# Negated scores with an exponential for each score map, and a later wait inside the transposes, in a hybrid attention and expert layer

## The reference, cut to what matters

```python
def diff_attention(q, k, v, lam):
    scale = dh ** -0.5                      # dh = 64, so an eighth
    ...
        s = jnp.einsum('bqhcd,bkhcd->bchqk', qblk, k).astype(F32) * scale
        p = jax.nn.softmax(s, axis=-1)
        a = p[:, 0] - lam * p[:, 1]
        return jnp.einsum('bhqk,bkhe->bqhe', a, vf)
```

## Time and profile before

| | us |
|---|---|
| three runs | 1222.29, 1220.74, 1217.69 |
| median | 1220.74 |
| the profiled execution, whole | 1222.5 |
| its span, first to last instruction | 1220.7 |
| PE busy in the span | 1082.9 (89%) |
| DVE busy | 595.6 (49%) |
| ACT busy | 404.4 (33%) |
| attention, half 0 | from 372 to 556 |
| attention, half 1 | from 641.7 to 783.3 |

### The profile page before, as it was taken

One profiled execution on the slowest core, in us unless ns is written; L12 is line 12 of the kernel. 1 busy time (PEld: TensorE's weight loads), 2 busy tenths in 40 slices (PEclk: granted clock), 3 DMA queues, 4 the chain that ended last, 5 costly groups with the idle time before them and its releaser, 6 DMA issues.

```text
span 1220.7 us, 13833 instructions
## 1 busy us (share of the span) xinstructions
PE 1082.9 (89%) x5427; PEld 776.9 (64%) x5427; DVE 595.6 (49%) x929; ACT 404.4 (33%) x799; POOL 103.5 (8%) x108
## 2 busy tenths in 40 slices
PE   4999999989998999999998899799994899777775
PEld 2687777777886777777876677687884333323322
DVE  4478525647335455451545665465639522222126
ACT  4441131112145555552236555431322111111103
POOL 1000011111000000000000101000014111111002
PEclk9999999989999999999999999899996899999998
DMA  9747723221421312313221211465519899999966
GB/s 307 264 165 259 261 97 108 83 61 52 147 87 36 111 53 65 109 52 129 70 86 53 63 56 52 165 262 192 209 47 333 350 420 420 420 421 419 418 269 239
DMA packets 72707, 226.17 MB, mean 185 GB/s; under 512 B 9534, under 2 KB 20087, under 8 KB 59331
## 3 DMA queue, kind: packets, MB, share of 16 engines
q1 hardware_dynamic: 65106, 208.35, 46.2%
q0 software_dynamic: 4464, 10.12, 2.2%
q10 hardware_dynamic: 3072, 6.82, 1.5%
HBM read 205.68 MB, written 25.72 MB: 190 GB/s over the span
## 4 chain that ended last, share of the span: by engine, by line
PE 66%; DVE 10%; issue 10%; ACT 9%; DMA 3%; SPq 1%; POOL 1%; ACTq 0%; DVEq 0%; POOLq 0%
PE ps L1084 36%; PE ps L1320 10%; PE ps L1333 5%; PE ps L1244 3%; ACT arena L1647 3%; DMA arena<-in_w_ada 2%; PE ps L1274 2%; PE ps L1038 2%; ACT w_high L1465 1%; PE ps L1258 1%; DVE mx L2122 1%; PE ps L1313 1%; DVE w_low L1825 1%; PE ps L1115 1%; DVE mx L2123 1%
## 5 line engine op out<-in xcount | busy, mean ns | idle before, releaser
L1084 PE MATMUL ps<-w_high,h_high 128*128 128x512 f32 x600 | 242.1, 403 | 5.4 <-DVE arena L1938 2.5
L1084 PE MATMUL ps<-w_high,h_low 128*128 128x512 f32 x600 | 235.8, 393 | 0.0
L1084 PE MATMUL ps<-w_low,h_high 128*128 128x512 f32 x600 | 235.7, 393 | 0.0
L1825 DVE TENSOR_TENSOR w_low<-w_loaded,w_high 128x2048 fp32r<-128x2048 f32 x44 | 100.7, 2289 | 105.9 <-ACT w_high L1465 105.9
L1320 PE MATMUL ps<-arena 128*64 128x512 f32 x512 | 120.0, 623 | 23.3 <-issue 22.0
L1084 PEld LDWEIGHTS ps<-w_high,h_high 128*128 128x128 f32 x600 | 114.1, 190 | 35.1 <-issue 6.4
L1084 PEld LDWEIGHTS ps<-w_high,h_low 128*128 128x128 f32 x600 | 113.9, 190 | 24.7
L1084 PEld LDWEIGHTS ps<-w_low,h_high 128*128 128x128 f32 x600 | 114.0, 190 | 22.7
L1465 ACT CAST w_high<-w_loaded 128x2048 fp32r<-128x2048 f32 x44 | 84.1, 1910 | 76.1 <-DMA w_loaded<-in_w_in 42.5
L1320 PEld LDWEIGHTS ps<-arena 128*64 128x64 f32 x512 | 41.7, 143 | 99.7 <-issue 99.7
L1575 ACT COPY arena<-ps 128x512 f32<-128x512 f32 x55 | 32.3, 587 | 168.8 <-PE ps L1084 168.8
(11 more groups left out here) (304 smaller groups left out, 1666.5 us busy)
## 6 DMA issues: line engine op xcount, KB each, us to landing
arena<-in_moe_w_down SPq DMA_DIRECT2D x32, 1024.0 KB, 25.5
arena<-in_moe_w_gate SPq DMA_DIRECT2D x30, 1024.0 KB, 21.0
arena<-in_moe_w_up SPq DMA_DIRECT2D x30, 1024.0 KB, 26.0
w_loaded<-in_w_in SPq DMA_DIRECT2D x27, 1024.0 KB, 6.0
arena<-in_w_ada SPq DMA_DIRECT2D x24, 1024.0 KB, 5.4
w_loaded<-in_w_in ACTq DMA_DIRECT2D x5, 1024.0 KB, 7.5
y_rows<-arena SPq DMA_DIRECT2D x10, 512.0 KB, 7.0
gates<-arena SPq DMA_DIRECT2D x20, 256.0 KB, 2.0
```

The costliest lines, as they stand in the source:

```text
L1084: mm = pe.matmul(out, x[:, t, kk * P:(kk + 1) * P], w[w_buf(i)][:, k, :], start=(begins and k == 0 and j == 0), stop=(k == HK - 1 and j == ...
L1825: dve.tensor_tensor(w_lo[b][:], w_raw[b], w_hi[b][:].bitcast(F32), ALU.subtract).then_inc(w_split, 1)
```

## The change

The transposed queries are copied out times minus an eighth, so both score maps are the negated, scaled scores. DVE takes the minimum of each map straight into the bias of its exponential, releases ACT after each of the two, and L2124 and the chained wait in front of it are gone. ACT waits for each map's own minimum and uses scale -1. On PE the wait for `pv_read` moves from in front of all six transposes to in front of the fifth; at t = 4, where there is one transpose, it stays where it was.

```diff
@@ PE, AT @@
                     if s:
                         pe.wait_ge(at_read, s)
-                        pe.wait_ge(pv_read, s)
+                        if t == PT:
+                            pe.wait_ge(pv_read, s)
...
                     for k in range(6 if t < PT else 1):
+                        if s and k == 4:
+                            pe.wait_ge(pv_read, s)
                         mm = pe.transpose(B(6 + k // 4)[:, (k % 4) * P:(k % 4 + 1) * P], mixed[:, k * P:(k + 1) * P], ident)
@@ ACT, the copies of the transposed queries @@
-                            ins = act.copy(qT[h % 2][:, 0:N512], src)
+                            ins = scale_copy(qT[h % 2][:, 0:N512], src, -DH ** -0.5)
...
-                            ins = act.copy(qT[h % 2][:, N512:N512 + P], src[:, 3 * P:4 * P])
+                            ins = scale_copy(qT[h % 2][:, N512:N512 + P], src[:, 3 * P:4 * P], -DH ** -0.5)
@@ ACT, E @@
-                    act.wait_ge(max_ready, s + 1)
                     if s:
                         act.wait_ge(mixed_ready, s)
                     for c in range(2):
+                        act.wait_ge(max_ready, 2 * s + c + 1)
                         act.activation(probs[:, c, 0:n], score[c][:, 0:n], ACT.Exp, bias=neg_mx[:, s % 2, c:c + 1],
-                                       scale=DH ** -0.5, accum_out=den[:, s % 2, c:c + 1]).then_inc(exp_done, 1)
+                                       scale=-1.0, accum_out=den[:, s % 2, c:c + 1]).then_inc(exp_done, 1)
@@ DVE, S @@
                     dve.wait_ge(pe_scores, s + 1)
-                    dve.tensor_reduce(mx[:, 0:1], score[0][:, 0:n], AXX, ALU.max)
-                    link(dve.tensor_reduce(mx[:, 1:2], score[1][:, 0:n], AXX, ALU.max))
-                    dve.tensor_scalar(neg_mx[:, s % 2, :], mx[:], -DH ** -0.5, None, ALU.mult).then_inc(max_ready, 1)
+                    for c in range(2):
+                        dve.tensor_reduce(neg_mx[:, s % 2, c:c + 1], score[c][:, 0:n], AXX, ALU.min).then_inc(max_ready, 1)
```

More of the change, by code:

```diff
@@ L300, in build @@
         var_e, ret_rstd = sb("var_e", [P, RH]), sb("ret_rstd", [P, RH])
-        mx, neg_mx = sb("mx", [P, 2]), sb("neg_mx", [P, 2, 2])
+        neg_mx = sb("neg_mx", [P, 2, 2])
         den, rden, coef = sb("den", [P, 2, 2]), sb("rden", [P, 2, 2]), sb("coef", [P, 2])
```

## The result

The changed kernel takes 1200.7 us (median of four runs, 1197.8 to 1202.7) against 1220.8 us; the ratio is 0.9845, with a 95% interval of 0.9821 to 0.9868. By this ratio it is 18.9 us less, and the two medians lie 20.1 us apart; 18.5 were forecast and 1202.2 us named. So the sum was right within what such a measurement can tell. Its terms were not all right, and the two profiled executions lie further apart than the medians: 1222.5 and 1197.8, or 24.7 us, since the one of after is the fastest of its runs and the one of before the slowest. Those 24.7 us can be followed in the two traces stretch by stretch. The last two columns are the difference and what the prediction had. It gave the walk's 13.5 us for half 1 as one number; here some 0.2 of it are put down to the first step, for the wait of 0.17 us that ended it before, and 13.3 to the others.

The account below looks back on a forecast made before the run. PE was taken to bound both halves of the attention, but in half 1 with waits from the DVE and ACT chain. 3.4 + 13.5 + 1.6 = 18.5 us off 1220.7 gave 1202.2 us, range 1197 to 1212.

Parts of the forecast that it names:

- the walk's 13.5 us: Half 1: stepping through its 20 steps with trace durations, the last six transposes begin at 761.6 instead of 775.15.
- Half 0, 3.4 forecast: Half 0: PE bounds it, so only its four stalls before transposes shrink, each by 0.84 us.
- 0.40 + 0.44: Each half 0 stall: square 0.40 us earlier through ACT's idle time, plus four transposes freed at 0.11 us each.
- 0.3 + 0.5 for the mixing: Half 1: what stays of the two transpose waits for the mixing, 2.2 us before.
- 0.9 + 0.25 for the square: Half 1: the longest wait for ACT's square, 1.72 us, keeps 0.9; the transposes after it keep 0.25.
- the slack of the steps before: Half 1: 0.45 to 0.9 us per earlier step makes up most of DVE's delay from a rounding's rest, 2.3 us.
- The clock: End of half 1: upper clock level for last transposes and the dense block after, 0.35 + 1.26 = 1.6 us.
- The moved wait has no price: Rival: on PE each of 32 moved waits costs 0.15 us and the clock still falls; 1208.6 us, chance 0.15.
- the overlap of exponential and minimum: Rival: first exponential and second minimum slow each other, both reading PSUM; gain 7.6, or 1213.1 us, chance 0.08.
- Nothing is given back: Rival: behind the attention, the expert weight stream sets the end and its start doesn't move; 1220.7 us, chance 0.07.
- The wait between fourth and fifth transpose empties nothing: Slower rival: that wait empties PE; at 1 us each the kernel takes 1234.2 us, chance 0.03.
- What should show it: Signs: no L2124, 1/sum wait about 0.9 us, no score waits for exponentials, half 0 stalls about 0.5, half 1 steps 6.83.

Follow-up runs that it names:

- The kernel with one release: Changed kernel, but ACT waits for both minima before the first exponential; 1215.1 us, ratio 0.9972 to the kernel before.
- the two experiments without the overlap: Kernel before with only the moved wait, 1217.45 us; changed kernel with ACT waiting for both minima before the first exponential, 1215.1 us.
- the first part alone: Changed kernel with the wait for the square back in front of all six transposes; 1203.1 us, ratio 0.9881 to the kernel before.

## Why the prediction was right, and where its terms were off

**What bounds the kernel.** Right. DVE's loop over ACT bounded the held steps of half 1, and with 1.01 us less PE does. The kernel with one release, which has everything but the overlap, loses 10.8 of the 12.15 us again.

**Half 0, 3.4 forecast, 3.94 found.** The mechanism was right, both terms were a little low: 0.50 + 0.50 a stall in place of 0.40 + 0.44. The first was read from the idle column, which leaves out that instructions overlap where no wait lies between them. The start times show it in the changed kernel:

```profile
400.20 0.38 ACT L1657 COPY arena<-ps 128x256 f32<-128x256 f32 x1
400.47 0.92 ACT L1650 ACTIVATE arena<-ps,neg_mx 128x768 f32<-128x768 f32 x1
```

These are 0.27 us from start to start; before, the copy started at 402.76 and the exponential at 403.54, 0.78 us. That is 0.51 earlier: the idle 0.40 and an overlap of 0.11. The page ScalarE: Activation LUTs of the Trainium skill (What ACT_TABLE_LOAD costs) gives about 93 ns for the overlap of two ACTIVATEs behind each other; the trace has 0.11 us for a copy and an exponential. Of the transposes' 0.50, four starts make 0.41 (the dense product begins 0.60 us after the first of six transposes and 0.19 after the first of two), and some 0.09 are the start behind the release. ACT's read of the square's sum, which releases them, starts at 410.92 and takes 0.22, and six transposes begin 0.14 us after its end, at 411.28. The pair behind the moved wait begins 0.06 us after it:

```profile
407.86 0.22 ACT L1667 ACTIVATION_READ_ACCUMULATOR ps<-ps,rden 128x1 f32 x1
```

The same is to be seen at the other stalls (0.15 before, 0.05 after).

**Half 1, step 1 to the last transposes, some 13.3 forecast, 12.15 found.** The step that failed is the size of the waits kept. They were put at 0.3 + 0.5 for the mixing and 0.9 + 0.25 for the square, and are these:

```profile
656.35 0.44 PE L1261 MATMUL ps<-const,arena 128*128 128x128 f32 x2 [0.76 <-ACT ps L1667]
...
661.92 1.09 PE L1261 MATMUL ps<-const,arena 128*128 128x128 f32 x6 [0.17 <-DVE arena L2137]
...
693.52 0.88 PE L1261 MATMUL ps<-const,arena 128*128 128x128 f32 x6 [0.79 <-DVE arena L2137]
...
754.81 0.88 PE L1261 MATMUL ps<-const,arena 128*128 128x128 f32 x6 [1.02 <-DVE arena L2137]
```

The square was sized rightly: 0.76 us at 656.35, and at 661.92 the six transposes take 1.09 us in place of 0.88, a gap inside the group that the list doesn't print. The mixing keeps 1.98 us in place of 0.8, and these 1.2 us are about the 1.15 missing. The walk gave the slack of the steps before a late one to DVE as if it could run ahead. It can't: it has no minimum to take before PE has made the map. DVE in the step before 693.52:

```profile
686.84 2.28 DVE L1828 TENSOR_TENSOR w_low<-w_loaded,w_high 128x2048 fp32r<-128x2048 f32 x1
689.04 1.81 DVE L2126 TENSOR_REDUCE neg_mx<-ps 128x1 f32<-128x768 f32 x2
...
692.45 1.02 DVE L2137 SCALAR_TENSOR_TENSOR arena<-arena,coef 128x768 f32<-128x768 f32 x1
```

The maps are there at 685.42 + 1.56 = 686.98, the rest of the rounding holds the minima until 689.04, and all of these 2.06 us reach the mixing, which ends at 693.47. PE asks for it early, as the score product in front is the short one of t = 4, begun at 692.24. The slack of the steps before was no reserve: it had gone into catching up. The maps of the step one earlier were ready at 678.61 + 1.56 = 680.17 and DVE came to them at 681.17. Two of the four roundings of half 1 (at 655.23 and 717.59) start late for another reason: DVE stands idle for 0.85 and 1.02 us until ACT has written its half. Halving the rounding took the waits for the mixing away, which bears the reading out.

**The clock.** The 1.6 us at the end of half 1 came as forecast (1.59): the last six transposes take 0.88 us in place of 1.20. In the two experiments without the overlap they take 1.54 and 1.13. Not forecast were two more places, the first step of half 1 (1.69 us, of which 0.2 were in the walk) and the stretch behind the attention (2.77 us). The table by stretches for both, the kernel before, then the changed one:

```profile
641.70:646.28 4.58, 4.58 (x15) 2.77 (x16) 1.99 (x3) 0.23 (x1) 0.00 (x0) 0.63 0.72 276
786.50:792.00 5.50, 5.39 (x13) 4.15 (x14) 1.32 (x2) 0.62 (x1) 1.09 (x1) 0.50 0.91 387
```

```profile
635.20:639.80 4.60, 4.54 (x22) 2.87 (x22) 1.85 (x3) 1.91 (x5) 0.00 (x0) 1.00 0.70 271
764.70:768.00 3.30, 3.30 (x17) 2.77 (x18) 1.20 (x2) 0.62 (x1) 0.97 (x1) 1.00 0.92 397
```

The granted clock was 0.63 and 0.50 there, the lower level for part or all of the stretch, and 1.00 after. Of the 2.77 us, 2.45 are in its first block of products (from its first product to the instruction behind its twelfth, 5.26 us before and 2.81 after). The same changed kernel, run again, has the first step at 4.59 us once more, but the block takes 768.65 - 764.55 = 4.10 us:

```profile
764.55 0.47 PE L1084 MATMUL ps<-w_high,od_high 128*128 128x512 f32 x1 [1.98 <-DVE od_low L1993]
...
768.65 0.92 PE L1115 MATMUL ps<-const,arena 128*128 128x128 f32 x4
```

So the block's whole gain is not the change's: of the seven traces with the overlap three have 2.8 us there and four have 4.1 to 4.4, the three without it 5.3. The first step is at 4.6 us in all seven and at 6.3 to 7.0 in the three without, and the last six transposes are at the upper level in all seven too, though in five of them the wait of 1.02 us in front stayed; of the idle time ahead of them only the score product's wait, 1.42 us before, went. That speaks for the change; but what PE does ahead of the first step is the same in both kernels (85.74 and 85.76 us), so how the change reaches that step stays open. Of the profiled pair's 24.7 us, 4.3 (2.77, and 1.69 less the forecast 0.2) lie in these places and 2.58 ahead of the attention, where nothing was changed. That leaves 17.9, and the forecast for what is left was 18.5. The nearness has some luck in it: half 0 gave 0.5 us more than forecast and half 1 1.15 less.

**The rivals.** The moved wait has no price that can be seen. Nor does the overlap of exponential and minimum: 0.90 us for an exponential either way. Nothing is given back: the first transposes of the experts start 23.72 us earlier (922.29 against 946.01), and from there to the end are 273.7 us, 274.7 before. The wait between fourth and fifth transpose empties nothing.

**What should show it.** L2124 gone, steps of 6.83 us, no wait of score products: as written. The wait of 1/sum was to fall to 0.9 us and fell to 1.14: I took the whole 1.07 off it, though 0.2 us of that are the multiply, which stood ahead of the wait. The stalls of half 0 were to show as 0.5 us and show as 0.20 and 0.26. With the first part alone 0.88 us of the 1.29 are left, and the moved wait brings them to 0.20: 0.68 less in the idle column, of which the step gains only 0.50. The column overstates this gain, as it understates the other.

## What to carry to other kernels

Where two engines make a chain by turns over several tiles, release the next engine for each tile, not for all: here one number in a wait was worth 10.8 us of 1220, as it took the chain below the length of the engine that should be the bound. Take the size of such an edit from start times, not from the idle column, and let an engine have slack only for work whose inputs are there. A wait that is satisfied may stand as late and as often as the hazards allow; moving one later frees what stands in front of it, but the gain arrives in full only where no other chain holds the loop.

## What the runs showed of the hardware that was not expected

- A satisfied semaphore wait between two transposes on PE costs nothing visible: 124 more of them left the two stretches at 168.34 and 114.97 us, against 168.39 and 115.02.
- ACT and DVE read two different pairs of PSUM banks at once without a visible price: an exponential of 128x768 takes 0.90 us with a minimum beside it for 0.77 us, and 0.90 us without.
- Of two ACT instructions the second starts 0.11 us before the first one's end where no wait lies between them; with a wait there this overlap is lost beside the wait itself.
- The same block behind the same short idle time (1.98 us before the first product of wd) ran at the upper clock level in three traces (2.8 us), in part at the lower one in four (4.1 to 4.4) and wholly in three (5.3); the same kernel gave 2.81 us in one trace and 4.10 in another. The page TensorE: Matmul & The Clock Gate of the Trainium skill (What's actually happening) tells that activity releases the throttle; no run here shows what decided between the two in this place.
